# The key numbers of the first dense tile: products, folds and sums made by GpSimd, compares left to VectorE

## The reference, cut to what matters

```python
q = (xb @ w_q).reshape(PEER_BLOCK, PEER_HEADS, 2, PEER_HALF)
s = jnp.einsum('thpd,hpnd->thpn', q, sub_keys)
s_top, i_top = lax.top_k(s, PEER_TOPK)                       # 16 of 128, for both key halves
cand = s_top[:, :, 0, :, None] + s_top[:, :, 1, None, :]
cand_idx = i_top[:, :, 0, :, None] * PEER_N_KEYS + i_top[:, :, 1, None, :]
best, pos = lax.top_k(cand.reshape(...), PEER_TOPK)
expert = jnp.take_along_axis(cand_idx, pos, axis=-1)         # the key numbers are looked up here
g = jax.nn.softmax(best, axis=-1)
act = jax.nn.gelu(jnp.einsum('td,thkd->thk', xb, u[expert]), approximate=False)
out = jnp.einsum('thk,thkd->td', g * act, v[expert])
```

## Time and profile before

| | us |
|---|---|
| median of 3 runs | 3162.53 |
| lowest and highest run | 3160.12, 3167.22 |
| the profiled execution's own time | 3156.35 |
| its span in the trace | 3154.5 |
| PE busy | 3039.2 (96%) |
| DVE busy | 2419.6 (77%) |
| ACT busy | 1342.8 (43%) |
| POOL busy | 1373.5 (44%) |

### The profile page before, as it was taken

How to read it: one execution, slowest core, us unless ns; L and a number is a source line. 1 busy time by engine, 2 the same in 40 slices (tenths; PEclk the granted TensorE clock), 3 DMA queues, 4 the chain that set the end, 5 groups by cost and what they waited for, 6 DMA issues and landing times. The chain is left out here.

```text
span 3154.5 us, 46000 instructions
## 1 busy us (share of the span) xinstructions
PE 3039.2 (96%) x16440; PEld 2035.4 (65%) x16440; DVE 2419.6 (77%) x5360; ACT 1342.8 (43%) x3425; POOL 1373.5 (44%) x1040
## 2 busy tenths in 40 slices
PE   8999999899999999999899998998999999999999
PEld 3467488766666666666344564887666666666664
DVE  6885469999899887867723264599998998888777
ACT  3332222786666555500111172227866665555100
POOL 0000000766676776767200000006676767767664
PEclk9999999899999999999999999999999999999999
DMA  9511352999999999999812201529999999999998
GB/s 312 196 54 41 127 200 76 378 338 409 408 408 394 409 409 409 409 409 409 341 62 87 86 8 40 214 75 342 331 410 409 408 399 404 409 409 409 409 409 352
DMA packets 282972, 931.24 MB, mean 295 GB/s; under 512 B 31837, under 2 KB 32493, under 8 KB 282233
## 3 DMA queue, kind: packets, MB, share of 16 engines
q0 software_dynamic: 147840, 536.96, 43.2%
q1 hardware_dynamic: 134904, 391.34, 32.7%
HBM read 921.87 MB, written 6.32 MB: 294 GB/s over the span
## 5 line engine op out<-in xcount | busy, mean ns | idle before, releaser
L810 PE MATMUL psum<-hT,mod 128*128 128x256 f32 x4096 | 959.4, 389 | 7.1 <-ACT big L1343 6.1
L810 PEld LDWEIGHTS psum<-hT,mod 128*128 128x128 f32 x4096 | 776.0, 194 | 126.0 <-issue 26.3
L1353 ACT ACTIVATE levels<-key_numbers,hT 128x128 bf16<-128x128 f32 x1792 | 567.2, 389 | 199.8 <-PE psum L866 199.4
L2102 DVE SCALAR_TENSOR_TENSOR tmp<-w,small,tmp 128x1024 f32<-128x1024 f32 x339 | 435.8, 1285 | 86.3 <-DMA w<-in_peer_up,tmp 39.4
L2281 POOL DMA_INDIRECT w<-in_peer_u,tmp x172 | 251.1, 1460 | 505.6 <-DVEq L1867 402.8
L2082 DVE CUSTOM_DVE_ANT_0 w<-w,hn 128x1024 f32<-128x1024 f32 x342 | 408.9, 1223 | 72.9 <-DMA w<-in_peer_down,tmp 37.9
L2281 POOL DMA_INDIRECT big<-in_peer_down,tmp x86 | 122.1, 1420 | 649.3 <-DVEq L1867 591.9
L820 PE MATMUL psum<-rows,big 128*128 128x512 f32 x752 | 337.1, 592 | 0.0
L866 PEld LDWEIGHTS psum<-x,levels 128*128 128x128 bf16 x6144 | 226.9, 103 | 163.8 <-issue 120.8
L1356 ACT ACTIVATE levels<-levels 128x512 bf16<-128x512 bf16 x448 | 282.3, 630 | 14.2
L2281 POOL DMA_INDIRECT w<-in_peer_down,tmp x170 | 238.0, 1400 | 107.4 <-DVE small L2082 65.1
(11 more groups left out here) (344 smaller groups left out, 4201.1 us busy)
## 6 DMA issues: line engine op xcount, KB each, us to landing
mod<-in_uT SPq DMA_DIRECT2D x256, 512.0 KB, 6.9
rows<-in_peer_v SPq DMA_DIRECT2D x64, 512.0 KB, 6.9
rows<-in_peer_up SPq DMA_DIRECT2D x64, 512.0 KB, 6.8
w<-in_w_in SPq DMA_DIRECT2D x14, 2048.0 KB, 7.9
srow<-in_peer_v SPq DMA_DIRECT2D x32, 512.0 KB, 7.0
tmp<-in_peer_v SPq DMA_DIRECT2D x32, 512.0 KB, 7.0
srow<-in_peer_up SPq DMA_DIRECT2D x32, 512.0 KB, 6.9
tmp<-in_peer_up SPq DMA_DIRECT2D x32, 512.0 KB, 7.2
```

Of the source, the lines that this page charges most:

```text
L810: last = nc.tensor.matmul(ps[4 + e % 2][:, 0:ND], ub[e % UV][:, k, :], hT[:, k, ND:SEQ], start=k == 0, stop=k == KC - 1)
L1353: last = nc.scalar.activation(hits[n % HITS][:, j * P:(j + 1) * P], keyno, ACT.Abs, bias=nibT[:, n * BATCH + j:n * BATCH + j + 1])
L2102: last = stt(y, row, c8[g % 2][:, b:b + 1], y, ALU.mult, ALU.add)
```

## The change

For tile 2 alone (`t == DENSE[0]`), in both layers, VectorE stops `numbers` after the two compares. They go to two one-hots of their own, in parts of `x` and `big` that are free at this time, with their own copies of the places and of the key numbers (`pool_first`, `pool_second`, `pool_tib`). After each compare `places_ready` is raised. GpSimd, in a new function `dense_numbers`, waits for it, and makes the product, the three folds and the last sum for each half, ten instructions in a chain, and raises `numbers_ready`. TensorE waits for it before it transposes tile 2's numbers, and VectorE before `numbers(0, 0, NH)`, which overwrites them. Tiles 3, 0 and 1 are as before.

```diff
@@ numbers(t, h0, h1), on VectorE
+                of_1, of_2, numbers_of = (pool_first, pool_second, pool_tib) if t == DENSE[0] else (of_first, of_second, tib)
...
+                if t == DENSE[0]:
+                    for m, of in enumerate((of_1, of_2)):
+                        shape = [P, TOPK, slots // 32, 32]
+                        step(tt(pool_onehot[m].rearrange("p (k r s) -> p k r s", k=TOPK, s=32),
+                                of.rearrange("p (r s) -> p r s", s=32).unsqueeze(1).to_broadcast(shape),
+                                place_no.unsqueeze(2).to_broadcast(shape), ALU.is_equal))
+                        dve.sem_inc(places_ready, 1)
+                    return
@@ peer(layer), on VectorE
                 dve.wait_ge(picks_turned, len(DENSE) * (layer + 1))
+                dve.wait_ge(numbers_ready, layer + 1)
                 at_once(numbers(0, 0, NH))
@@ turn_picks(layer, n), on TensorE
                 pe.wait_ge(picks_ready, len(DENSE) * layer + n + 1)
+                if n == 0:
+                    pe.wait_ge(numbers_ready, layer + 1)
@@ GpSimd
+            def dense_numbers(layer):
+                add, step, slots = nc.gpsimd.tensor_tensor, Chain(pool, c_numbers), SLOTS
+                step.n = layer * 10
+                tib4 = pool_tib.rearrange("p (m k h) -> p m k h", m=2, h=NH)
+                pool.wait_ge(x_stored, 16 * NT * (layer + 1))
+                for m, dst in enumerate((ia[0], ib[0])):
+                    pool.wait_ge(places_ready, 2 * layer + m + 1)
+                    oh = pool_onehot[m]
+                    oh4 = oh.rearrange("p (k j h) -> p k j h", k=TOPK, h=NH)
+                    step(add(oh4, oh4, tib4[:, m].unsqueeze(2).to_broadcast([P, TOPK, TOPK, NH]), ALU.mult))
+                    for k in (8, 4, 2):
+                        step(add(oh[:, 0:k * slots], oh[:, 0:k * slots], oh[:, k * slots:2 * k * slots], ALU.add))
+                    step(add(dst, oh[:, 0:slots], oh[:, slots:2 * slots], ALU.add))
+                pool.sem_inc(numbers_ready, 1)
+
             for layer in range(2):
+                dense_numbers(layer)
                 for n in range(4 * GROUPS):
```

More of the change, by code:

```diff
@@ L377, in build @@
         gT = part(top_, 3, 1)
+        pool_first, pool_second = [part(big, 16 + 0.25 * n, 0.25, BF16) for n in range(2)]
+        pool_tib = part(big, 16.5, 0.5, BF16)
+        pool_onehot = [part(x_, 12, 4, BF16), part(big, 17, 4, BF16)]
         y_dense = [psum[:, n * D:(n + 1) * D] for n in range(len(DENSE))]
@@ L452, in build @@
         picks_ready = sem("dense_picks_ready")
+        places_ready, numbers_ready = sem("places_of_dense_tile_ready"), sem("numbers_of_dense_tile_ready")
+        c_numbers = sem("numbers_step")
         picks_turned = sem("dense_picks_turned")
@@ L1820, in numbers @@
                 oh = (wide_onehot if count == NH else onehot)[:, 0:slots * TOPK]
-                tib4 = tib[:, 2 * at:2 * (at + slots)].rearrange("p (m k h) -> p m k h", m=2, h=count)
+                of_1, of_2, numbers_of = (pool_first, pool_second, pool_tib) if t == DENSE[0] else (of_first, of_second, tib)
+                tib4 = numbers_of[:, 2 * at:2 * (at + slots)].rearrange("p (m k h) -> p m k h", m=2, h=count)
                 of_ti = ti[t][:, 2 * at:2 * (at + slots)].rearrange("p (h m k) -> p m k h", h=count, m=2)
@@ L1834, in numbers @@
                 step(tt(row_at[:, c], row_at[:, c], row_to[:, c], ALU.min), 1)
-                step(nc.vector.tensor_copy(by_place(of_first), by_head_(row_no)))
-                step(tt(by_place(of_second), by_head_(bp[t]), by_head_(row_at), ALU.subtract))
+                step(nc.vector.tensor_copy(by_place(of_1), by_head_(row_no)))
+                step(tt(by_place(of_2), by_head_(bp[t]), by_head_(row_at), ALU.subtract))
+                if t == DENSE[0]:
[6 more added lines that the diff above has]
+                    return
                 yield
-                for m, (of, dst) in enumerate(((of_first, ia), (of_second, ib))):
+                for m, (of, dst) in enumerate(((of_1, ia), (of_2, ib))):
                     shape = [P, TOPK, slots // 32, 32]
```

## The result

The changed kernel takes 3177.12 us (median of 7 runs, 3171.63 to 3184.94) against 3163.62 us of the kernel before (7 runs, 3160.12 to 3167.22): ratio 1.0043, 95% interval 1.0031 to 1.0055. It is slower by 13.5 us. The forecast was 3180, and slower.

What follows compares the result with a forecast made beforehand. VectorE's chain to the first gather was taken as the bound: 15.1 us lost less 6.2 gained is 8.9 a layer, 17.8 in all, giving 3174.2, or 3180 against the median of 3162.53; 8-in-10 range 3157 to 3190.

Steps and rivals of the forecast that it cites:

- What bounds: VectorE's chain from the choice to the first gather sets both expert stages' start; 1 us delays everything behind by 1 us.
- What is removed, 6.20 us: Product, folds and sum of tile 2's two key halves leave VectorE's chain, 3.10 us each; added semaphores taken at nothing.
- The cap, 1.9 and 1.4: Most that could arrive per layer before VectorE waits for ScalarE's exponentials: 1.9 us in the first, 1.4 in the second.
- GpSimd's price, 16.7 us at 2.1 ns a value: Time of GpSimd's ten instructions over 7936 values per partition, both key halves of tile 2, in each layer.
- ScalarE's row: ScalarE's copy of 512 values in 1073 ns, 2.1 ns a value, taken as GpSimd's price.
- The lock: During tile 3's numbers, a GpSimd instruction reading SBUF holds VectorE's two-input instructions for its whole length, and the reverse.
- VectorE's loss, 15.1 us: Holds per layer during tile 3's numbers: GpSimd's 16.7 us less 1.6 us running beside it; 8.9 us later net.
- TensorE's stalls: TensorE waits for late VectorE: 4.4 us at the transposes, then 9.8 us before the first gate products.
- (a): Rival: GpSimd works beside VectorE and holds nothing; 2 to 3.3 us less, 3160; chance 0.18.
- (b): Rival: lock present but GpSimd cheap, 0.6 to 1.2 ns a value; −3 to +4 us, 3159 to 3167; chance 0.13.
- (c): Rival: GpSimd slow, 4.2 ns a value; 25.5 us a layer, +51, 3214; chance 0.05.
- (d): Rival: more than the cap arrives through changed interlocking over the stages; over 6.3 us faster, 3155 or less; chance 0.05.

Runs made afterwards that it cites:

- e1_idle: The changed kernel with GpSimd's ten instructions taken out (tile 2's key numbers left out), waits, semaphores and moved buffers kept; ratio 0.9992, median 3160.21 us.
- e5_open: e2_late with ScalarE's exponentials of tiles 2 and 3 made earlier and TensorE transposing after two dense blocks, not three; ratio 0.9995, median 3160.27 us.
- e2_late: The changed kernel with places_ready raised only after tile 3's numbers, so GpSimd's ten instructions lie beside tile 0's top 16; ratio 0.9991, median 3160.42 us.
- e4_half: The changed kernel with only tile 2's first key half on GpSimd, the second on VectorE as before; ratio 1.0028, median 3170.80 us.

## Why the prediction was right, point by point

- **What bounds:** right. VectorE's chain to L1883 (L1867 before) sets the start of both stages, and the table gives about 1 us for 1 us in both directions, within 2 to 5 us. Places in the second layer move by the first layer's delay as well: the first gather there came at 2155.75, where 2148.3 was named, which had counted one layer's 8.9 us only; two make 2157.2.
- **What is removed, 6.20 us:** right; in e1_idle the chain to `start_gates` is 6.0 us shorter. The new semaphores cost about 0.1 us each, not nothing: 0.15 us lie behind each compare, where 0.03 lay.
- **The cap, 1.9 and 1.4:** right, 1.76 and 1.19 in e1_idle; e5_open shows it by moving it.
- **GpSimd's price, 16.7 us at 2.1 ns a value:** 16.4 us undisturbed in e2_late (3.63 + 4.15 + 0.43, and 3.64 + 4.15 + 0.42), 1.8 ns a value for the products and 2.3 for the folds. That ScalarE's row came so near is luck: it is no reason for GpSimd's speed.
- **The lock:** right in kind. It was argued from GpSimd's waits in the earlier trace rows, the direction that rows could show. Of these two gathers the one of 1.72 us carries the reading, against 0.94 in the earlier trace rows; the one of 1.02 is hardly longer. The other direction stands in the rows of the changed kernel, and e1_idle, e4_half and e2_late confirm it. What holds what was too simple: it is not two-input instructions alone (next point).
- **VectorE's loss, 15.1 us:** mis-sized, 13.1. I had counted only 1.6 us of VectorE's work as lying beside GpSimd's, the single-input instructions. That split was wrong: L1832, L1834 and L1838, single-input, were held for 2.15, 1.17 and 3.62 us, while L1831, L1833, L1839 and L1843, which came just as one of GpSimd's instructions had ended, kept their lengths. Net 7.18 us by the start of tile 0's top 16, where 8.9 was forecast: 2 × 1.7 = 3.4 us too much. The forecast change was 17.8 us and 13.5 came; that 3180 lies only 3 us above 3177 owes 1.1 us to the median of the kernel before, 3162.53 then and 3163.62 over all its runs.
- **TensorE's stalls:** 4.4 us at the transposes was forecast, 0.88 + 0.70 came. The first transposes need only tile 2's gates, which VectorE ends 1.25 us before tile 3's, and at this place VectorE was 6.8 us late, not 8.9. The 9.8 us before the gates were 10.13, close by luck: the delay of 8.9 and the 4.4 taken off it were both too large (6.84 and 1.58).
- **The rivals:** (a), nothing held, is refuted by the rows above; (b) and (c) by 1.8 to 2.3 ns a value. (d) did not occur.

## What to carry to other kernels

Work moved from VectorE to GpSimd is not taken off VectorE as long as it runs beside VectorE's two-input instructions or TENSOR_SCALARs: here 6.2 us removed brought 13.1 us of holds. The same ten instructions beside MAX8, FIND_INDEX8 and MATCH_REPLACE8 cost 2.9 us in the first layer, all of it in the two-input L1810 between them; where the work lies decides, and one semaphore moved it. Before costing such a move, look for the next late input behind the relieved engine as well: here 6.2 us of relief were worth 1.8 and 1.2 until ScalarE's exponentials and TensorE's transposes had been moved too.

## What the runs showed of the hardware that was not expected

A TENSOR_SCALAR over 128 fp32 or uint32 values, with one input, 0.22 us when alone, took up to 3.62 us beside GpSimd's product, and 1.90 us beside a memset that reads nothing, while a two-input instruction beside the same memset kept its 0.29 us. VectorE's holds are inside the instruction's own duration in the trace, not in an idle time before it: it looks busy, 2434.4 us for 2419.6, with 20 instructions fewer. And GpSimd's memset of 2048 bf16 values took about 1.8 us, half of the 3.64 of a two-input product over as many.
